# Attention stage of a hybrid encoder layer: three sets of subtractions made by GpSimd in place of VectorE

## What is computed

```
z = einsum('bqhd,bkhd->bhqk', qi, k) * scale
log_1m = where(valid, log_sigmoid(-z), 0.0)
suffix = cumsum(log_1m, axis=3, reverse=True) - log_1m
a = where(valid, exp(log_sigmoid(z) + suffix), 0.0)
attn = einsum('bhqk,bkhd->bqhd', a, v)
...
mix = concatenate([pool_out, attn], axis=-1) @ w_out
```

## Time and profile before

| | |
|---|---|
| median of 3 runs | 864.76 us (864.37 to 865.07) |
| profiled execution, its own time | 863.53 us |
| its span, first to last instruction | 861.8 us |
| PE busy | 792.0 us, 92% of the span |
| DVE busy | 597.8 us, 69% |
| ACT busy | 349.7 us, 41% |
| GpSimd busy | 314.2 us, 36% |
| mean granted clock of TensorE | 0.968 of full |
| `block_b` begins | 237.4 us from the span's start |
| its first `mix` begins | 321.03 us |

### The profile page before, as it was taken

The page is one execution under the profiler, slowest core; times in us unless marked ns, Lnnn a source line. Parts: engine busy times, 40 slices in busy tenths (PEclk is TensorE's granted clock), DMA queues, the critical chain, the costliest instruction groups (busy, mean ns, idle before and its releaser), DMA issues. The chain is left out here.

```text
span 861.8 us, 13448 instructions
## 1 busy us (share of the span) xinstructions
PE 792.0 (92%) x4805; PEld 625.4 (73%) x4806; DVE 597.8 (69%) x685; ACT 349.7 (41%) x645; POOL 314.2 (36%) x259
## 2 busy tenths in 40 slices
PE   3899999999978899999999995599999999999894
PEld 2689999999945566766767784378888888888641
DVE  6679679852079965875777566998557998563097
ACT  3811110111156763444444435544544444444144
POOL 3000799960000001000000001257665897663156
PEclk9999999999999999999999996699999999999897
DMA  8956544630073501321102037798779998889594
GB/s 322 397 175 204 163 152 132 200 98 2 1 257 144 144 17 50 100 72 38 62 26 74 25 122 265 279 327 278 272 253 334 401 384 289 278 306 345 175 355 157
DMA packets 77362, 165.32 MB, mean 192 GB/s; under 512 B 7397, under 2 KB 32517, under 8 KB 75266
## 3 DMA queue, kind: packets, MB, share of 16 engines
q1 hardware_dynamic: 68402, 132.15, 44.2%
q0 software_dynamic: 7760, 28.31, 9.3%
q10 hardware_dynamic: 1152, 4.19, 1.4%
HBM read 132.57 MB, written 32.08 MB: 191 GB/s over the span
## 5 line engine op out<-in xcount | busy, mean ns | idle before, releaser
L2101 PE MATMUL psum<-we_hi,x_parts 128*128 x384 | 137.5, 403 | 1.4 <-DVE we_lo L1724 1.1
L1724 DVE TENSOR_TENSOR we_lo<-we_raw,we_hi 128x2048 fp32r<-128x2048 f32 x48 | 116.1, 2422 | 1.5
L1723 DVE CAST we_hi<-we_raw 128x2048 fp32r<-128x2048 f32 x44 | 60.7, 1379 | 47.9 <-DMA we_raw<-in_w_down_dram 24.5
L449 PE MATMUL psum<-hn_hi,w_hi 128*128 128x364 f32 (+1 forms) x384 | 90.7, 331 | 1.3 <-issue 0.7
L449 PE MATMUL psum<-hn_lo,w_hi 128*128 128x364 f32 (+1 forms) x384 | 90.1, 329 | 0.0
L449 PE MATMUL psum<-hn_hi,w_lo 128*128 128x364 f32 (+1 forms) x384 | 89.9, 328 | 0.0
L2101 PEld LDWEIGHTS psum<-we_hi,x_parts 128*128 128x128 f32 x384 | 72.1, 188 | 16.5 <-issue 2.3
L1040 PE MATMUL psum<-wo_hi,mixin 128*128 128x512 f32 (+1 forms) x256 | 83.2, 396 | 0.6 <-DVE logits L1367 0.6
L2101 PE MATMUL psum<-we_lo,x_parts 128*128 x192 | 75.2, 392 | 0.0
L633 DVE SCALAR_TENSOR_TENSOR proj<-wm,cT,proj 128x2048 f32<-128x2048 f32 x28 | 72.6, 2638 | 0.1
L449 PEld LDWEIGHTS psum<-hn_hi,w_hi 128*128 128x128 f32 x384 | 67.0, 189 | 5.7 <-issue 4.8
(11 more groups left out here) (334 smaller groups left out, 1587.3 us busy)
## 6 DMA issues: line engine op xcount, KB each, us to landing
we_raw<-in_w_up_dram SPq DMA_DIRECT2D x32, 1024.0 KB, 8.4
wm<-in_w_mod_dram SPq DMA_DIRECT2D x16, 1024.0 KB, 5.3
we_raw<-in_w_down_dram SPq DMA_DIRECT2D x16, 1024.0 KB, 6.6
w_raw<-in_w_in_dram SPq DMA_DIRECT2D x16, 512.0 KB, 6.2
we_raw<-ff_d SPq DMA_DIRECT2D x12, 512.0 KB, 8.3
proj<-in_x_prompt_dram SPq DMA_DIRECT2D x4, 1024.0 KB, 8.1
sc_room<-in_w_mod_dram SPq DMA_DIRECT2D x4, 1024.0 KB, 14.0
proj<-in_w_mod_dram SPq DMA_DIRECT2D x2, 2048.0 KB, 12.2
```

Of the source, the lines that this page charges most:

```text
L449: mm = pe.matmul(psum[:, 3 * slot + c, 0:n], w[:, slot, k, :], hn[:, k, t0:t0 + n], start=(k == 0 and w is w_hi and hn is hn_hi), stop=(k ...
L1723: then(dve.tensor_copy(we_hi[:, a:b], raw))
L1724: dve.tensor_tensor(we_lo[:, a:b], raw, we_hi[:, a:b].bitcast(F32), ALU.subtract).then_inc(ready, 1)
L2101: mm = pe.matmul(psum[:, bank, :], x[:, s, k, :], w[:, bass.ds(at + k * 2 * DE, 2 * DE)], start=(k == 0 and x is x_hi and w is we_hi), sto ...
```

## The change

GpSimd makes the `dv_old` subtraction as soon as the cached rows are there, then planes 2 and 3 of the prompt rows' differences with their first column, then the eight low halves of the output weights, each behind the ACT step that makes its high half. DVE keeps planes 0 and 1 of the prompt rows. `dv_ready` counts three producers now. GpSimd waits for all nine turned value tiles (`v_turned`) and for the saved edge columns (`b_dve`) before it overwrites its planes. Its wait for `rows_in`, the DMA of zeros and the small tables come behind all that.

```diff
 DVE_BESIDE = {
-    2: "TV:0", 3: "DV:0", 5: "TV:1", 7: "TV:2", 9: "TV:3", 10: "TV:4", 12: "TV:5 wl:0", 13: "wl:1 TV:6 wl:2",
-    14: "wl:3", 15: "TV:7", 16: "TV:8 wl:4", 17: "wl:5", 18: "wl:6", 19: "wl:7", 26: "Pl:0", 28: "C0:0",
+    2: "TV:0", 3: "DV:0", 5: "TV:1", 7: "TV:2", 9: "TV:3", 10: "TV:4", 12: "TV:5", 13: "TV:6",
+    15: "TV:7", 16: "TV:8", 26: "Pl:0", 28: "C0:0",
...
@@ gpsimd @@
+            pool.wait_ge(b_const, CONSTS)
+            pool.wait_ge(cache_loaded, CACHE_LOADS)
+            pool.tensor_tensor(dv_old[:, :, :], v_sh, dv_old[:, :, :], ALU.subtract).then_inc(old_ready, 1)
+
+            pool.wait_ge(b_dve, edges_kept)
+            pool.wait_ge(v_turned, TILES)
+            pool.tensor_tensor(vT[:, 2:4, 1:SEQ][:, :, ::-1], vT[:, 2:4, 0:SEQ - 1][:, :, ::-1],
+                               vT[:, 2:4, 1:SEQ][:, :, ::-1], ALU.subtract).then_inc(b_const, 1)
+            pool.wait_ge(b_const, CONSTS + 1)
+            pool.tensor_copy(vT[:, 2:4, 0], edge[:, 2:4, 0]).then_inc(dv_ready, 1)
+
+            def low_wo(k):
+                pool.wait_ge(wo_hi_ready, k + 1)
+                raw = wo_raw[:, k, :]
+                pool.tensor_tensor(wo_lo[:, k, :], raw, wo_hi[:, k, :].bitcast(F32), ALU.subtract).then_inc(wo_split, 1)
+
+            for k in range(KC):
+                low_wo(k)
             pool.wait_ge(rows_in, 16 * 5)
-            pool.wait_ge(b_const, CONSTS)
@@ tensor @@
-                pe.wait_ge(dv_ready, 2 if n else 1)
+                pe.wait_ge(dv_ready, 3 if n else 1)
@@ vector @@
-                if u == 1:
-                    dve.wait_ge(cache_loaded, CACHE_LOADS)
-                    dve.tensor_tensor(dv_old[:, :, :], v_sh, dv_old[:, :, :], ALU.subtract).then_inc(old_ready, 1)
...
-                        differences(0, SEQ)
-                        dve.tensor_copy(vT[:, :, 0], edge[:, :, 0]).then_inc(dv_ready, 1)
-                    elif step == "wl":
-                        low_wo(n)
+                        differences(0, SEQ, 2)
+                        dve.tensor_copy(vT[:, 0:2, 0], edge[:, 0:2, 0]).then_inc(dv_ready, 1)
```

More of the change, by code:

```diff
@@ L812, in block_b @@
         POOL_PIECES = ((0, 512), (512, 512), (SEQ, DEC))
-        gather_made = 1
+        gather_made, edges_kept = 1, 2
         sample_units = sum(u[0] == PT for u in units)
@@ L921, in _ @@
             pool.memset(ones[:, :], 1.0).then_inc(b_const, 1)
-            pool.wait_ge(b_const, CONSTS + 1)
+            pool.wait_ge(b_const, CONSTS + 2)
             pool.affine_select(out=tri[:, :], in_=ones[:, :], compare_op=ALU.is_gt, fill=0.0, base=0,
@@ L1237, in stage_v, with differences @@
                 dve.tensor_copy(v_st[0:rows(t), t, :], psum[0:rows(t), v_bank(n), :]).then_inc(dve_staged, 1)
-            def differences(lo, hi):
-                then(dve.tensor_tensor(vT[:, :, lo + 1:hi][:, :, ::-1], vT[:, :, lo:hi - 1][:, :, ::-1],
-                                       vT[:, :, lo + 1:hi][:, :, ::-1], ALU.subtract))
+            def differences(lo, hi, planes):
+                v = vT[:, 0:planes, :]
+                then(dve.tensor_tensor(v[:, :, lo + 1:hi][:, :, ::-1], v[:, :, lo:hi - 1][:, :, ::-1],
+                                       v[:, :, lo + 1:hi][:, :, ::-1], ALU.subtract))
             then(dve.tensor_reduce(gather[:, :], ident[:, :].rearrange("p (g j) -> p j g", j=32), AX_X, ALU.add))
@@ L1249, in _ @@
             then(dve.tensor_tensor(edge[:, :, 1], vprev[:, :], vT[:, :, SEQ], ALU.subtract))
+            assert step_.n == edges_kept
             stage_v(0)
-            differences(SEQ, NT)
+            differences(SEQ, NT, 4)
             dve.tensor_copy(vT[:, :, SEQ], edge[:, :, 1]).then_inc(dv_ready, 1)
@@ L1284, in copy_dv @@
                 dve.tensor_copy(dv[0:r, j, :], bank("TV", n)[0:r, :]).then_inc(dv_copied, 1)
[L1286 to L1289, removed]
             def low_mix(n):
```

## The result

| | before | after |
|---|---|---|
| median of 4 runs each, side by side | 864.64 us (864.37 to 865.07) | 873.15 us (870.71 to 876.92) |
| ratio, 95% interval | | 1.0106 (1.0085 to 1.0127) |
| profiled execution, its span | 863.53 us, 861.8 | 870.71 us, 869.0 |
| granted clock of the profiled execution, mean | 0.968 | 0.972 |

The change makes the kernel slower by 8.5 us. The forecast was 872.8 us.

The account below looks back on a forecast made before the run. DVE was taken to set the pace up to 297 us, with PE behind it. Part 1's +3.0 and part 2's +5.0 gave +8.0 us on 863.53, so 871.5, or 872.8 us against the median; range 859.5 to 881.

Parts of the forecast that it names:

- The exclusion: GpSimd and DVE instructions with two SBUF inputs, scans included, keep each other out for the whole instruction; PSUM copies run free.
- Rival 1: Scans aren't kept out by GpSimd, so the change is faster: 859.5 us; chance 0.17.
- Rival 2: Backwards reading costs double (+3.8), PSUM copies are held too (up to +5), PE's clock may drop; all 882; chance 0.20.
- Rival 3: GpSimd finds gaps between scans, half of its 27 us runs beside other work: 864.8 give or take 1; chance 0.07.
- The prices: GpSimd's times: cached rows 4.7 us, each low half 2.36, prompt half 3.8 or twice that, first-column copy under 0.6, hidden.
- Part 1: 245 to 262 us: iteration 1's scans wait for GpSimd's cached-rows subtraction, PE's turning comes later by +1.7 or +4.4; taken +3.0.
- the second branch: Iteration 1: GpSimd goes in between the two scans, PE's transposes move to 256.4 and the turning to 264.1, +4.4 us.
- Part 2: 272 to 297 us: each iteration needs two scans plus one GpSimd subtraction, 30.5 against 25.0 us: +5.5, taken as +5.0.
- PE's slack: Behind iterations 12 to 19, some half a microsecond of slack on PE takes a little off the +5.5 us.
- The rest costs nothing: GpSimd's DMA of zeros and tables come up to 10 us later, last low half before 306; the output weights' load isn't later.

Follow-up runs that it names:

- the fills: Kernel before, all DVE work kept, plus 16 GpSimd zero fills of unread room behind the weights' high halves, reading nothing: 863.5 us, ratio 0.9986.
- the subtractions: Kernel before, all DVE work kept, plus eight GpSimd subtractions of two SBUF tensors into unread room behind the high halves: 880.92 us, ratio 1.0174.
- A: Kernel before with the eight low halves left on DVE, spread over iterations 14, 16, 18, 20, 22, 24, 25, 27: 862.63 us, ratio 0.999.

## Why the prediction was right, and where it was off

**The direction and the mechanism were right.** The exclusion that I took from a single subtraction and a single power holds for scans: 2.44 us became 5.32, 5.39 and 8.38 in three kernels. For the first two the end of GpSimd's instruction and the scans' own 2.44 give 5.51 and 5.58, so the records are 0.2 us shorter than that. That it is the reading, and not GpSimd's being at work, is shown by the fills against the subtractions. The Trainium skill ("SBUF — State Buffer", two separate sides) states it in this form: the shared ports go to one of the two for a whole instruction, and VectorE's instructions with two SBUF inputs are blocked only by a GpSimd instruction that reads SBUF. The runs agree on both halves, +17.6 us with reads and none with fills, except for the 0.2 us by which the records are shorter than a lock for the whole instruction would have them.

**Rival 1**, scans not held out, fell with that. **Rival 2** fell in two of its three parts: the prompt half, read backwards, took 3.60 us, not 7.6, and a copy out of PSUM kept 0.68 us beside GpSimd. Its third part, the clock behind longer gaps, which it left without a price, is seen once more in the changed kernel, 0.87 from 284 to 297 us for 1.00; what it cost there isn't told apart. **Rival 3**, that it evens out, holds for one part in three: the cached rows alone, 1.0005.

**The prices** held: 4.52 us for 4.7; 2.37 at the shortest for 2.36; 3.60 for 3.8. The copy of the first column took 1.00 us, and 2.17 with the prompt half alone, for "under 0.6", and was hidden both times. The Trainium skill ("GPSIMD Engine Reference", elementwise side by side) has 4497 ns for 2048 columns with two inputs. The cached rows agree with it at 4.52; the prompt half, one tensor read at two places, would be 4.49 us for 2046 columns by an estimate from that figure, and was 3.60 in the kernel that makes this part alone.

**Part 1** was a choice between two branches, +1.7 and +4.4, and I took the middle, 3.0, which no mechanism gives. The trace shows the second branch: GpSimd entered between the two scans, as the earlier trace rows had it. The branch's steps read 256.4 for the transposes and 264.1 for the turning, measured are 255.58 and 263.50, and PE's own work between them 7.9 us for 7.7. No row of before gives that 7.7: there the same work takes 7.3 us, 10.03 from 249.68 to 259.71 less waits of 2.44 and 0.32. The changed kernel's 7.9 came with a lower clock, 0.60 from 256 to 262 us for 0.88, so the term held partly by luck. The row that decided between the branches stood in the prediction; the step that was off is the taking of a middle.

**Part 2** was 5.5 us and measured 4.4. The bound of one subtraction and two scans for each iteration was a little too strict from iteration 12 to 16, 13.42 us where it says 14.2. Two things show in the timelines. The fourth subtraction ran on until 290.37, past the start of iteration 16's scans at 290.01, so 0.36 us of it are paid in the next stretch. And GpSimd's first three took 7.74 us with a whole pair of scans in between, where 3 x 2.36 + 1.27 makes 8.35: some 0.2 us of each instruction run beside the other engine's. From 16 to 20 it is 15.99 for 16.3.

**PE's slack** was taken off with 0.5 us, and 1.0 had to be added. I had read PE as the bound from 297 on the earlier trace rows; behind the change the late scan pairs hold it up to 306 us. Its values of 306.23, behind a wait of 1.17 us, start 0.23 us after iteration 20's scans. Before, the same instructions stood 0.87 us ahead of those scans:

```profile
296.82 0.88 PE L1028 MATMUL psum<-aT_room,dv 128*64 128x128 f32 x12
```

So PE enters the stretch that it bounds 1.1 us later relative to DVE, which fits the +1.0 of the account; the low halves alone have the same +1.0 there.

The first `mix` came 9.4 us later and not 8.0, and the median's 8.5 us lies between that and the 7.2 us of the profiled execution. That 872.8 and 873.15 are so near is in part luck: the terms were off by +0.9, -1.1 and +1.5 us, the clock gave some back, and the four runs behind the median lie 6.2 us apart. "The rest costs nothing" held: GpSimd's DMA of zeros went out at 304.97, its tables were done by 307, and the output weights' load started at 253.82, where it was at 253.87.

What the sum lacked as a term is **PE's clock behind a gap**. A wait of DVE that opens a PE gap can cost more than its own length where PE is the bound behind it. With the prompt half alone the medians differ by 3.35 us where 1.5 to 2 were expected, and the trace shows PE at 0.50 and without a wait there. That the gap brought the low clock about is likely but argued, since the same stretch had it for nearly as long in one kernel whose gap was as before.

What stays open: why GpSimd's subtraction, and not the second scan, got in when the first scan ended, while its copy of two columns did not in the kernel with the prompt half alone; how much of PE's low clock around 252 to 262 us each edit brings about; and what makes A, and now and then the kernel before, fall into two groups of times.

## What to carry to other kernels

GpSimd is not a second VectorE: in these runs its instructions that read SBUF shut out, wherever they met them, VectorE's instructions with two SBUF inputs, scans among them, for all but some 0.2 us of its length. So price such a move by GpSimd's duration less the part that runs beside VectorE's copies out of PSUM or its gaps, and expect a gain only if that is less than what VectorE sheds; fills can go there for nothing. Where VectorE sets the pace in one stretch and has room in the next, move its work in time instead: eight subtractions, spread over more iterations, gave 2.4 to 2.6 us where moving them to GpSimd lost 6.6. And look at TensorE's granted clock behind every gap that an edit opens or shifts, since that can cost more than the gap; and take more than one execution before an edit is blamed for it, as the same stretch came up to 2 us later with nothing changed.

## What the runs showed of the hardware beyond that

- Between two scans that stand back to back on DVE a waiting GpSimd subtraction got in: the pair of 8.38 us, against 5.32 where GpSimd had nothing more queued. It isn't always so: with the prompt half alone GpSimd's copy of 128x2, issued at 250.64, when the first scan had only just been let in, ends at 252.81, with the pair (252.83).
- A GpSimd copy with one input, 1.04 us for 1024 columns, holds scans and subtractions out as well: pairs of 2.10 and 2.58 us for 1.27 and 1.79, subtractions of up to 1.82 for 1.21.
- GpSimd's instruction was cheaper where both inputs are one tensor, shifted: 3.60 us for 2046 columns backwards (1.76 ns a column) against 4.51 us for 2048 from two tensors (2.2 ns). Reading backwards cost nothing visible.
- Around PE gaps the granted clock fell to the level of 1.2 GHz and stayed there for some time of dense work: 0.50 from 252 to 262 us with the prompt half alone (gaps of 3.12 and 2.04 us), and 0.50 from 260 to 272 behind the 3.80 us with the cached rows' subtraction moved. Behind the unchanged gap of 2.44 us it differed between executions, 0.50 from 252 to 260 with the low halves alone and 0.52 and 0.63 from 254 to 258 in before. Runs of one and the same kernel before spread from 862.25 to 869.29 us.
